# Sixteen and twenty-four taps of a depthwise convolution moved from GpSimd to VectorE

## The reference, cut to what matters

```python
def conv_mixer(p, w_dw, b_dw, g_ln, b_ln):
    a, gt = jnp.split(p, 2, axis=-1)
    u = a * jax.nn.sigmoid(gt)
    y = lax.conv_general_dilated(u, w_dw[:, None, :], window_strides=(1,),
                                 padding=[(CONV_KERNEL // 2, CONV_KERNEL // 2)],   # 31 taps
                                 feature_group_count=CONV_WIDTH) + b_dw            # 256 channels
    return jax.nn.silu(layernorm_f32(y, g_ln, b_ln)).astype(p.dtype)

# in each layer
px = split_cols(hx @ w_in[l])          # latent tokens; pc likewise for the context
c_x = conv_mixer(px[8], w_dw[l], b_dw[l], g_conv_ln[l], b_conv_ln[l])
x = x + mod_x[2] * (jnp.concatenate([m_x, d_x, c_x], axis=-1) @ w_out[l])
if not last:
    c_c = conv_mixer(pc[8], ...)       # the context is convolved in layer 0 only
```

## Time and profile before

| | us |
|---|---|
| three runs | 1527.35, 1527.25, 1524.26 |
| median | 1527.25 |
| profiled execution, its own time | 1524.21 |
| its span, first to last instruction | 1522.4 |
| PE busy | 1422.1 (93%) |
| VectorE busy | 958.2 (63%) |
| ScalarE busy | 639.9 (42%) |
| POOL busy | 353.9 (23%) |
| mean granted TensorE clock | 0.981 |

### The profile page before, as it was taken

The page is one execution under the profiler, slowest core; times in us unless marked ns, Lnnn a source line. Parts: engine busy times, 40 slices in busy tenths (PEclk is TensorE's granted clock), DMA queues, the critical chain, the costliest instruction groups (busy, mean ns, idle before and its releaser), DMA issues.

```text
span 1522.4 us, 20407 instructions
## 1 busy us (share of the span) xinstructions
PE 1422.1 (93%) x7624; PEld 1134.8 (75%) x7624; DVE 958.2 (63%) x1375; ACT 639.9 (42%) x1033; POOL 353.9 (23%) x272
## 2 busy tenths in 40 slices
PE   5999999669999999999999999987999999999996
PEld 3787787334478888888878897576878878878885
DVE  4654655654464444343468584645888887987986
ACT  3443334451220110010025344525676676676775
POOL 1049999910100000000011999400000000000000
PEclk9999999889999999999999999999999999999999
DMA  9344444321232222222324133408979778877950
GB/s 366 140 166 166 166 167 150 127 83 59 81 116 106 87 108 87 107 79 97 115 84 160 62 112 115 162 1 357 368 283 357 292 282 336 314 278 317 337 200 28
DMA packets 30881, 267.06 MB, mean 175 GB/s; under 512 B 3424, under 2 KB 3552, under 8 KB 4960
## 3 DMA queue, kind: packets, MB, share of 16 engines
q1 hardware_dynamic: 30816, 266.15, 46.2%
HBM read 265.09 MB, written 1.05 MB: 175 GB/s over the span
## 4 chain that ended last, share of the span: by engine, by line
PE 67%; POOL 13%; DVE 7%; ACT 6%; issue 4%; DMA 2%; ACTq 0%; DVEq 0%; SPq 0%
PE ps L501 32%; PE ps L904 13%; POOL sb_arena L1979 7%; PE ps L924 7%; POOL sb_arena L1982 6%; PE ps L785 4%; PE ps L874 2%; DVE sb_rows_n L1672 1%; DMA sb_arena<-mod 1%; PE ps L519 1%; PE ps L883 1%; PE ps L508 1%; DMA sb_arena<-in 1%; ACT sb_x_r L1267 1%; PE ps L659 1%
## 5 line engine op out<-in xcount | busy, mean ns | idle before, releaser
L501 PE MATMUL ps<-sb_h_hi,sb_w_hi 128*128 128x512 f32 (+1 forms) x640 | 242.1, 378 | 5.5 <-DVE sb_w_lo L1443 3.6
L501 PE MATMUL ps<-sb_h_hi,sb_w_lo 128*128 128x512 f32 (+1 forms) x640 | 239.7, 375 | 0.0
L501 PE MATMUL ps<-sb_h_lo,sb_w_hi 128*128 128x512 f32 (+1 forms) x640 | 239.6, 374 | 0.0
L1979 POOL TENSOR_SCALAR sb_arena<-sb_arena,sb_small 128x512 f32<-128x512 f32 (+1 forms) x120 | 184.8, 1540 | 11.8
L501 PEld LDWEIGHTS ps<-sb_h_hi,sb_w_hi 128*128 128x128 f32 x640 | 121.3, 189 | 30.0 <-DVE sb_w_lo L1443 4.7
L904 PE MATMUL ps<-sb_egu_lo,sb_h_lo 128*128 128x512 f32 (+1 forms) x384 | 143.4, 373 | 0.0
L1982 POOL TENSOR_TENSOR sb_arena<-sb_arena 128x512 f32<-128x512 f32 (+1 forms) x120 | 139.1, 1159 | 10.0
L1442 DVE CAST sb_w_hi<-sb_arena 128x2048 fp32r<-128x2048 f32 (+1 forms) x39 | 46.7, 1198 | 145.0 <-PE ps L501 120.1
L501 PEld LDWEIGHTS ps<-sb_h_hi,sb_w_lo 128*128 128x128 f32 x640 | 121.1, 189 | 21.7
L501 PEld LDWEIGHTS ps<-sb_h_lo,sb_w_hi 128*128 128x128 f32 x640 | 121.3, 190 | 20.6
L1825 DVE TENSOR_TENSOR sb_egu_lo<-sb_arena,sb_con_r 128x1024 fp32r<-128x1024 f32 x98 | 115.4, 1220 | 31.1 <-ACT sb_con_r L1267 31.0
(11 more groups left out here) (313 smaller groups left out, 2973.6 us busy)
## 6 DMA issues: line engine op xcount, KB each, us to landing
sb_arena<-experts SPq DMA_DIRECT2D x90, 1536.0 KB, 8.8
sb_arena<-mod SPq DMA_DIRECT2D x48, 1024.0 KB, 5.2
sb_arena<-in SPq DMA_DIRECT2D x24, 1024.0 KB, 6.2
sb_arena<-gate SPq DMA_DIRECT2D x11, 1024.0 KB, 4.8
sb_arena<-up SPq DMA_DIRECT2D x11, 1024.0 KB, 5.0
sb_arena<-out SPq DMA_DIRECT2D x8, 1024.0 KB, 4.8
sb_arena<-down SPq DMA_DIRECT2D x8, 1024.0 KB, 4.8
sb_arena<-down SPq DMA_DIRECT2D x4, 768.0 KB, 4.2
```

The source lines that it names most:

```text
L501: ins = pe.matmul(o, left[a], right[b], start=(k == first and n == 0), stop=(k == final and n == len(PRODUCTS) - 1))
L1979: g.tensor_scalar(p, u, w[:, j:j + 1], None, ALU.mult)\
```

## The change

VectorE takes the first taps of channel tile 1: 16 of them in layer 0 and 24 in layer 1, an equal share (two or three) at the end of each of the eight chunks n = 4 to 11. On VectorE a tap is one instruction, since its `scalar_tensor_tensor` multiplies and adds, and each waits for the one before. POOL does tile 0 as before, then waits for VectorE's last tap and does the other 15 (layer 1: 7) taps of tile 1. In layer 1 the step of the convolution's mean goes from 6 to 4, and the seven filling products ahead of it go.

```diff
-CONV_STEP = (10, 6)
+CONV_STEP = (10, 4)
+DVE_TAPS = (16, 24)
...
-        ("heads", 0): 0, ("heads", 1): 5, ("scores", 0): 5, ("scores", 1): 0, ("conv", 0): 0, ("conv", 1): 7,
+        ("heads", 0): 0, ("heads", 1): 5, ("scores", 0): 5, ("scores", 1): 0, ("conv", 0): 0, ("conv", 1): 0,
...
                     memory_step(l, step)
+                    each = DVE_TAPS[l] // (len(IN_ORDER) - MEMORY_FROM)
+                    conv_taps(l, range(each * (n - MEMORY_FROM), each * (n - MEMORY_FROM + 1)))
                 memory_step(l, step + 1)
...
+            def conv_taps(l, taps):
+                s0 = low(l) // CTX
+                w = par("w_dw", l).rearrange("p (m j) -> p m j", m=2)[:, 1]
+                y = cy[:, 1, :].rearrange("p (s t) -> p s t", s=2)[:, s0:2]
+                dve.wait_ge(*dve_drained.at(("ca", l, 1)))
+                for j in taps:
+                    u = upad[:, 1, s0:2, j:j + SEQ]
+                    if j == 0:
+                        ins = v.tensor_scalar(y, u, w[:, 0:1], par("b_dw", l)[:, 1:2], ALU.mult, ALU.add)
+                    else:
+                        dve.wait_ge(*dve_done.at(("tap", l, j - 1)))
+                        ins = v.scalar_tensor_tensor(y, u, w[:, j:j + 1], y, ALU.mult, ALU.add)
+                    ins.then_inc(*dve_done.tick(("tap", l, j)))
...
-                    for j in range(TAPS):
+                    first = DVE_TAPS[l] if m else 0
+                    if m:
+                        pool.wait_ge(*dve_done.at(("tap", l, first - 1)))
+                        pool.wait_ge(*pool_done.at(("tap", l, 0, TAPS - 1)))
+                    for j in range(first, TAPS):
                         u = upad[:, m, s0:2, j:j + SEQ]
-                        if j:
+                        if j > first:
                             pool.wait_ge(*pool_done.at(("tap", l, m, j - 1)))
```

## The result

| us | before | changed |
|---|---|---|
| median, 5 runs each | 1527.25 (1524.26 to 1530.21) | 1515.83 (1514.32 to 1517.60) |
| ratio, 95% interval | | 0.9933 [0.9915, 0.9951] |
| profiled execution, its own time | 1524.21 | 1515.78 |
| its span | 1522.4 | 1514.0 |

A forecast was written before the change was run, and what follows sets the result against it. TensorE was taken to bound the kernel, with POOL's taps on the chain where TensorE waits for them in layer 0. Terms -17.4 + 2.1 - 3.0 = -18.3 gave 1505.9, raised to 1507 us; range 1500 to 1513.

The forecast's parts named there:

- Layer 0, POOL: Attention of layer 0: POOL's last taps end at 290.9, so TensorE's 15.55 us wait before the mean goes whole.
- Layer 0, the clock: Mean of layer 0: without the idle stretch it runs at full clock, 1.87 us more gained.
- Layer 0, the price on VectorE: Projection of layer 0: 16 taps, two a chunk, fit in VectorE's idle stretches and cost nothing.
- Layer 1, the price on VectorE: Projection of layer 1: three taps ahead of one chunk's weights make TensorE wait, +2.1 us, from 1.2 to 6.
- the second triple: Projection of layer 1: the next three taps, behind the late weights, delay VectorE by an amount that just fits its slack.
- Layer 1, attention: Attention of layer 1: earlier mean without filling products and Silu ahead of the last transposes save 3.0 us, bounds 0 to 6.5.
- Rival 3: Attention of layer 1 gives nothing or loses 2, loads and scaling each ending last: 1511 us; chance 0.1.
- Half the spread of the runs: Half of the 3.0 us by which the profiled execution was under the median, added to 1505.9 to forecast 1507.
- 1: Layer 0's wait for POOL stays in part, its last fifteen taps starting later or running slower: 1510 us; chance 0.12.
- 2: VectorE bounds layer 1's projection, each tap meeting a lock: 6 to 8 us instead of 2.1, 1512 us; chance 0.13.
- 4: Slower than before: VectorE's last layer 0 tap comes 18 us late, handing over to POOL late: 1530 us or more; chance 0.03.
- 5: The wait at layer 0's mean was never POOL's, so the change does not do what it says; chance 0.02 with others.

The follow-up runs named there:

- e1: Changed kernel with layer 1 as before the change (all taps on POOL, mean at step 6, seven filling products); only layer 0 changed: 1512.97 us, ratio 0.9926.
- e2: Kernel before the change with only the 24 taps of layer 1 moved to VectorE, mean at step 6 and filling products kept: 1529.31 us, ratio 1.0025.
- e10: Changed kernel with 21 layer 0 taps on VectorE, three in each of the first seven chunks; layer 1 without VectorE taps or filling, mean at step 6: 1509.06 us.
- e14: The same kernel as e10, run again in another job with five rounds: 1502.75 us, ratio 0.9866.
- e4: Changed kernel plus four filling products ahead of TensorE's wait for the weights of head 1, second direction, in layer 1: 1516.73 us, ratio 0.9938.
- e6: Changed kernel with layer 1's taps shared as 6, 3, 0, 3, 3, 3, 3, 3 and its mean at step 6, no filling products: 1509.03 us, ratio 0.9884.
- e7: As e6, but with the seven filling products ahead of layer 1's mean, as before the change: 1513.32 us, ratio 0.9927.
- e3: Changed kernel with the three taps of layer 1's third chunk moved to its first chunk, mean still at step 4: 1513.65 us, ratio 0.9931.
- e5: As e3, but with the mean of layer 1 at step 5 instead of 4: 1516.58 us, ratio 0.9933.
- e9: Changed kernel with layer 0's 16 taps as 2, 3, 2, 3, 2, 2, 2, 0; layer 1 without VectorE taps or filling, mean at step 6: 1507.71 us.

## Why the prediction was right in sign and wrong in size

The sum said -18.3 and the profiled execution has -8.4. Of the 9.9 us between them 3.3 are missing in the attention of layer 0, 3.2 in the projection of layer 1, 3.2 in its attention and 1.8 at the end, less 1.6 that came ahead of the projection of layer 0 and is not of the change. The first two terms stayed inside their own bounds and were mis-sized: what a fallen clock costs was left out of both. The third lies outside its bounds (0 to 6.5 us of gain), and there the mechanism was wrong.

**Layer 0, POOL: right as a mechanism, too large as a number.** POOL ended at 288.24 (I had said 290.9), no wait stood before the mean, and it was 1.88 long. That it started at 293.99 where I had said 293.7 is partly luck: from the first scores it came at 47.67, 1.9 us later than the 45.7 at which TensorE asked before, and the early start of the layer hid that. And 15.55 us of wait were taken from one execution, where a second showed 9.76.

**Layer 0, the clock: the first step that failed.** I counted 1.87 us for a mean at full rate and nothing against it. They came, and 1.40 of them went again behind the wait at 313.51. There was more of that kind. With a wait of 15 us ahead of the mean, whatever TensorE lost between 248 and 294 us cost nothing. Without it each of these losses counts. In nine profiled executions with the same two taps a chunk in layer 0 the mean comes 47.4 to 52.3 us behind the first scores, and it goes by the mean granted clock of that stretch: 47.4 to 47.7 in the four with 0.93, 50.9 to 51.1 in the three with 0.83, 52.3 in the two with 0.80. A0 is 87.6 to 93.4. From 261 us to the mean the changed kernel has a clock of 1.00, e1, with the same code there, 0.85.

```profile
261.00:294.00 33.00, 27.12 (x217) 16.63 (x218) 28.06 (x76) 20.38 (x63) 25.70 (x18) 1.00 0.37 131
```

```profile
261.00:299.00 38.00, 32.29 (x221) 19.68 (x221) 29.60 (x76) 20.69 (x65) 25.83 (x18) 0.85 0.34 114
```

So the term is -10 to -16 with a mean of these nine of 91.4, 12.0 under the one execution of before (8.6 under e2's); my lower bound of 12 was meant for a late POOL and missed this. Why one execution has the lower clock and another of the same code not, no run shows. I had asked when the cover fails for VectorE's taps, and not for the clock.

**Layer 0, the price on VectorE: right for the projection** (203.87 us before, 203.84 after), wrong behind it: 2.7 us later at the memory heads, since POOL's additions now meet VectorE's small instructions there. That they meet because POOL's taps start when VectorE's end is likely (all nine executions have it) but was not tested by itself. e10 and e14 show that these 2.7 us are to be had back.

**Layer 1, the price on VectorE: the place right, the term mis-sized.** I had given 2.1, from 1.2 to 6. The wait is 1.85 (2.1 forecast) and stands where I put it, and the second triple just fitted, as said. The other 3.5 us are the half clock behind the wait (e4 takes most of it away without touching the taps). I had kept the clock for the attention alone.

The rule of the Trainium skill, "SBUF — State Buffer", section "Who interferes with whom", that two engines exclude each other for the whole instruction, stood beside the rival of 6 to 8 us. It came for one tap in three. The three taps took 2.20 against 1.6 bare. The first met an addition of POOL (0.74 us from 862.84) and took 1.06; the other two stood beside a product and took 0.58 and 0.49. So the trace agrees with the rule for POOL's additions, as it does in layer 0 where the instruction of two inputs at 245.95 ended 0.03 us behind one, and not for POOL's products: in the changed kernel's trace none of the 84 held a VectorE instruction to its end.

**Layer 1, attention: the mechanism was wrong.** -3.0 was forecast, +0.2 measured. Leaving out the filling products was worth 3.0 (e6 against e7); that the sum said 3.0 too is luck, since it gave it to the move of the mean. Moving the mean from step 6 to 4 costs: 1.0 over e6 in e3, 3.3 in the changed kernel, where the clock was lower. I had listed its items (load, scaling, Silu), but set them against VectorE's idle 6.51 us as if one were paid by the other. They were not: root and scaling stand ahead of a combination for which TensorE then waits 3.58 us (in e3 and e4 too), its products behind it take nearly twice as long, and VectorE's idle time stands at the end with 8.84 us. Rival 3, "the loads and the scaling each ending last", is what came.

**The end, not priced: +1.8.** It lies between the output projection and the experts' first product: 32.86 us, where before has 31.09. The same products (L874, now L875) take 5.46 us instead of 3.84, at a lower clock.

```profile
1046.90 3.84 PE L874 MATMUL ps<-sb_kq,sb_H 128*128 128x128 f32 x32 [2.27 <-DVE sb_kq L1801]
1036.83 5.46 PE L875 MATMUL ps<-sb_kq,sb_H 128*128 128x128 f32 x32 [2.62 <-DVE sb_kq L1819]
```

e3, e4 and e5 have this stretch at 32.9 too, the other eleven at 31.0 to 31.4. None has an edit there, but the four (with the changed kernel) are those with the mean at step 4 or 5 and the root two steps behind it. So it is probably a further price of that move, by way of the clock; how, no run shows. (e9's 1.7, and as much of e5's 3.4, is another loss, inside the output projection.)

**Half the spread of the runs** (+1.1 on 1505.9) was a choice without a row behind it, and too little: single executions of one kernel stand up to 9 us apart.

Of the other rivals, 1 didn't come (no wait was left ahead of the mean) and 2 came at one chunk only. 4 and 5 didn't come: VectorE's last tap ended at 241.08, 2.5 sooner than costed, and the wait was POOL's.

## What to carry to other kernels

A long wait covers all small losses ahead of it. When you remove it, add up what TensorE lost to a low clock and to short waits in the stretch that it covered, and take that off the gain. Look also at more than one execution of the kernel before, since the wait itself may differ from one to the next (here 15.55 and 9.76 us). A new wait in a full projection may cost more than itself, here 1.85 us and 3.5 of half clock behind it: look first for a chunk that can do without the new instructions (here one of eight). And undo an edit's parts one at a time: here one part of three brought the gain, another cost, and the gain of the third came from a line beside the one that was meant.

## What the runs showed of the hardware that was not expected

- POOL's same 62 taps of layer 0, behind each other, took 211.4 us in one execution and 209.1 in another; with TensorE's own arrival the wait for them was 15.55 and 9.76 us.
- VectorE instructions of 128x16 and 128x4, 0.17 us each at their shortest, took 1.26 and 1.15 us, each to the end of one addition of POOL; the second took 0.40 beside one of its products. Of three taps of 128x256 (0.49 bare) the one that met an addition took 1.06, the two beside a product 0.58 and 0.49.
- The same wait of TensorE for a combination in layer 0, 2.90 and 2.91 us, was followed by products at full clock before the change and at half clock after it. In the attention of layer 0, executions of the same code had a mean clock of 0.80, 0.83 or 0.93 up to the mean, and took 52.3, 51.0 or 47.5 us for it.
- Filling products move the half rate, they don't take it away: five at the start of layer 0's attention left out, kept, or put into the wait gave 89.01, 88.79 and 89.38 us.
